# FNet/gMLP encoder layer on eight cores: earlier release of the first w_in cast and of group 1's x, row scales half a step back in the A loops, channel blocks moved on, one more merge add on VectorE

## The chip, the cores and the metric

One Trainium2 chip, 8 cores, each running the same program on its own sequences (cores 0 to 3: one prompt sequence of 2048 positions and one sample sequence of 4096; cores 4 to 7: three prompt sequences of 2048). No core talks to another. The metric is the device time in microseconds (us) of the slowest core; the outputs have to agree with the reference.

## What is computed

One layer of a trunk, cut to what matters here (per sequence of S positions, D = 1024):

```python
mod = silu(c) @ w_ada + b_ada                  # "adaLN": (B, 3D)
shift, scale, gate = split(mod, 3)
h = rmsnorm(x, norm_g) * (1 + scale) + shift
z = h @ w_in                                   # 4608 columns
a, ga, u, v, gb, ma, mb = split(z)             # 512 each, ma and mb 1024 each
y_a = fourier(a) * silu(ga)                    # real part of a 2-D DFT over (positions, 128 channels), 128x128 map per group
y_b = u * chunk_mix(layernorm(v)) * silu(gb)   # w_s over 128 positions
merged = sigmoid(ma) * (y_a @ w_pa) + sigmoid(mb) * (y_b @ w_pb)
y = rmsnorm(x + gate * (merged @ w_out), final_g)
```

## The kernel before

All five instruction streams are written out by hand in one program order: a small scheduler (`Sched`) appends each operation to its engine's stream and adds the semaphore waits that its reads and writes of 512-byte granules ask for. An engine runs its own stream strictly in that order, so where an operation stands in the program decides what it can hold up. The DMA queues are the streams of SyncE (x, tables, Gd, outputs), ScalarE (w_ada, at the start) and GpSimd (every weight that is cast from float32 to bfloat16 on its way: w_in by sections `w_sec`, w_pa, w_pb, w_out).

Each core has 48 blocks of 128 rows for the Fourier branch ("A") and 12 tiles T = 0 to 11 of 512 rows for the rest.

**Start.** ScalarE issues w_ada as eight 1 MB blocks (kc 0 to 7, `wada_off`). SyncE loads the first four x blocks, then waits for a block of w_ada before it loads four more (L876). GpSimd waits for a block of w_ada before it casts section 0 of w_in (L376). TensorE multiplies the eight w_ada blocks in order (L885), transposes group 0 of x (`fe_t`, L447), and the modulation tables come out (L896, L899); `fe_e` (L460 on VectorE, L465 on ScalarE) writes hT of group 0.

**A loops.** `ABlock.body` runs over groups q of four row blocks j. For each: `a_proj` (eight matmuls L490, VectorE copies the result, L313), then the first DFT stage of the block before it (`pend`: one matmul L500, copy alternately on ScalarE and VectorE, L313 or L311, write to Gd by SyncE, L503). At j = 2 comes `fe(q+1)`: 32 transposes that read all four scaled rows of the next group, then `fe_e`. At j = 0 and j = 2 stand one `sc(n)` and one `sq(n)`. n counts half groups (two row blocks): `sq(n)` squares two rows on ScalarE (L421) and takes the reciprocal root on GpSimd (L408, L410); `sc(n)` scales the two rows on VectorE (L427) and then has SyncE load the next rows into the ring slots that it has read. Object A has 4 groups in its loop (and two more groups, 4 and 5, that feed tiles 0 and 1; `A.fe(5)` stands behind the loop), a ring of 8; A2 has 8 groups (and one more), a ring of 6, and runs after tile 3.

**Channel blocks.** The second DFT stage reads Gd back (`g2_load`, L523) and has 4 blocks for the first sequence (`s3s`, `s3_single`, L560, L568) and 8 for the others (`s3j`, `s3_joint`, L535, L545). They are placed between the products of `silu_section` of the tiles (L680, Silu on ScalarE, L708) by its argument `between`. After tile 0's GA section `channel_tables` (L381 to L395) reads tables that `late_tabs` loads on SyncE's queue behind the reads of Gd; the casts of w_in sections 6, 7, 8, w_pa, w_pb and w_out follow on GpSimd's queue.

**Merge.** For each of eight blocks dmc `merge` makes two products (L772, L778), two multiplies on VectorE (L775, L781) and an add (L783): on GpSimd for dmc 0 to 6, on VectorE for dmc 7. In tile 1 and in tiles 4 and 8, GpSimd also multiplies the rows of w_out by the gate (`gate_mul`, L675) during the merge. `out_chunk` (L607) needs all eight merged blocks and all of w_out.

Of the kernel before, what the change touches and what calls it, by code (L numbers as in the profile page):

```python
# [210 lines left out]
def build_nc():  # L211
# [163 lines left out]

    w_sec(0, after=gk(wada_off[6], 512))  # L376

# [389 lines left out]

    def merge(tb, dmc):
        sl = tb.sigs.pop(dmc)
        mk = gk(tb.m + 1024 * dmc, 1024)  # L770
        b = newbank()
        S.pe([lambda e, k=k: e.matmul(ps[b][:], lhsT=w_pa_sb[:, k, dmc * 128:(dmc + 1) * 128], rhs=tb.sga[:, k, :],  # L772
                                      start=(k == 0), stop=(k == 3)) for k in range(4)],
             reads=gk(tb.a, 4096) + wpak, writes=[("ps", b)])
        S.op("dve", lambda e: e.tensor_tensor(out=tb.mg[:, dmc, :], in0=ps[b][:], in1=bv(sl[0], 512), op=ALU.mult),  # L775
             reads=[("ps", b)] + gk(sl[0], 1024), writes=mk)
        b2 = newbank()
        S.pe([lambda e, k=k: e.matmul(ps[b2][:], lhsT=w_pb_sb[:, k, dmc * 128:(dmc + 1) * 128], rhs=tb.sgb[:, k, :],  # L778
                                      start=(k == 0), stop=(k == 3)) for k in range(4)],
             reads=gk(tb.b, 4096) + wpbk, writes=[("ps", b2)])  # L780
        S.op("dve", lambda e: e.tensor_tensor(out=bv(sl[1], 512), in0=ps[b2][:], in1=bv(sl[1], 512), op=ALU.mult),  # L781
             reads=[("ps", b2)] + gk(sl[1], 1024), writes=gk(sl[1], 1024))
        S.op("pool" if dmc < 7 else "dve", lambda e: e.tensor_tensor(out=tb.mg[:, dmc, :], in0=tb.mg[:, dmc, :], in1=bv(sl[1], 512), op=ALU.add),  # L783
             reads=mk + gk(sl[1], 1024), writes=mk)


    class ABlock:
# [46 lines left out]
        def body(self, hooks):  # L834

            for q in range(self.nq):
                for j in range(4):
                    if j == 2:
                        self.fe(q + 1)
                    st1 = a_proj(self.dst[q][0], j, self.f, 4 * q + j, self.N1)  # L840
                    if self.pend:
                        self.pend.pop(0)()
                    self.pend.append(st1)
                    if j % 2 == 0:
                        self.sc(2 * q + j // 2 + 4)
                        self.sq(2 * q + j // 2 + 5)
                if q in hooks:
# [28 lines left out]
    tabs = []  # L876
    A.load_to(8, after=gk(wada_off[7], 512))
    for n in range(2):
# [27 lines left out]
    A.sc(2)  # L906
    A.sq(4)
    A.sc(3)
    A.body(hooks1)

    def s3_begin(f):
# [25 lines left out]
    silu_section(T0, SEC["GB"], T0.sgb, T0.b)  # L937
    silu_section(TB1, SEC["GB"], TB1.sgb, TB1.b, lambda fc: s3s(fc // 2) if fc % 2 == 0 else None)
    silu_section(T0, SEC["GA"], T0.sga, T0.a, lambda fc: s3s(2 + fc // 2) if fc % 2 == 0 else None)
    channel_tables()  # L940
# [3 lines left out]
    w_sec(8)  # L944
    silu_section(TB1, SEC["GA"], TB1.sga, TB1.a)
    w_out_load()
# [25 lines left out]
    for dmc in range(8):  # L972
        if dmc + 1 < 8:
            merge_gates(TB1, dmc + 1)
        merge(TB1, dmc)
        if dmc < 7:
# [27 lines left out]
    for T in range(2, NT):  # L1004
# [32 lines left out]
        after(0)  # L1037
        silu_section(tb, SEC["GB"], tb.sgb, tb.b, s3j if T == 4 else None)
        after(1)
        silu_section(tb, SEC["GA"], tb.sga, tb.a, (lambda fc: s3j(4 + fc)) if T == 4 else None)  # L1040
        after(2)
# [15 lines left out]
        for dmc in range(8):  # L1057
            if dmc + 1 < 8:
                merge_gates(tb, dmc + 1)
            if t == 0 and dmc < 7:  # L1060
                for k in ((0, 1) if dmc == 0 else (dmc + 1,)):
                    gate_mul(O_WIN, k)
            merge(tb, dmc)
            if T == 2 and dmc < 5:
# [40 lines left out]
        elif isA:  # L1105
            A2.fe(0)
            A2.sq(3)
            out_chunk(tb, T, 0, OS[0])
            A2.sc(3)
            A2.sq(4)  # L1110
            out_chunk(tb, T, 1, OS[1])
# [140 lines left out]
```

How the kernel before makes its waits and increments, by code:

```python
        def run(stream, e):  # L1130
            for it in stream:
                if it[0] == "wait":
                    e.wait_ge(sems[it[1]], it[2])
                elif it[0] == "raw":
                    it[1](e)
                else:
                    ins = it[1](e)
                    ins.then_inc(sems[it[2]], it[3])
```

## Time and profile before

| what | value |
|---|---|
| timed runs of the kernel | 1278.76, 1279.31, 1287.62 us, median 1279.31 |
| profiled execution | 1272.01 us, its span 1270.5 us (core 7, the slowest; the others 1264.0 to 1269.6) |
| busy, core 7 | PE 1222.7 us (96%), DVE 627.7 (49%), ACT 483.2 (38%), POOL 349.5 (28%) |
| mean granted TensorE clock | 0.992 to 0.995 of full on all cores |
| HBM | 143 MB read, 31 MB written, 138 GB/s over the span |

PE is TensorE's matmuls, PEld its weight loads, DVE VectorE, ACT ScalarE, POOL GpSimd, SP SyncE; a name with q (SPq) is the engine's queue, where DMAs are issued. The span runs from the first to the last instruction; the time of an execution is a little longer. A matmul's duration in the rows holds some 0.17 us of pipeline behind its last column, so the next one starts before it ends. L680 is line 680 of the kernel.

### The profile page before, as it was taken

Reading aid. Unit: us, or ns where it says so; the run is one execution under the profiler, and the core shown is the slowest. Engines: PE = TensorE matmul, PEld = TensorE weight load, DVE = VectorE, ACT = ScalarE, POOL = GpSimd, SP = SyncE. Lnnn points to the kernel's source line nnn. Section 1 sums busy time; section 2 is a strip of 40 time slices with the busy share of each in tenths; the row PEclk is TensorE's granted clock in tenths of the full one; section 3 lists DMA queues with packets and bytes.
Section 4 is the critical chain, followed back from the end, with each engine's and each line's share of the span. In section 5 each row is a group of like instructions: output and inputs, shape, how many; then the busy total and the mean of one; then the engine's idle time right before and its main releaser. Section 6 shows DMA issues by size and latency. Waiting matters only on the chain.

```text
span 1270.5 us, 19981 instructions; the slowest of 8 cores (1264.0 to 1270.5 us)
## 1 busy us (share of the span) xinstructions
PE 1222.7 (96%) x6504; PEld 587.9 (46%) x6504; DVE 627.7 (49%) x945; ACT 483.2 (38%) x818; POOL 349.5 (28%) x430
## 2 busy tenths in 40 slices
PE   6798999999999999989999999999999999999997
PEld 1354454444444455545444444444444444444443
DVE  0383265364756578844435434443446444344434
ACT  1483312323423368743332333243323423333322
POOL 0221132730522332203713213213128122132121
PEclk9899999999999999999999999999999999999999
DMA  8999895234426297656312212121262112121111
GB/s 273 265 254 186 167 170 164 67 116 147 156 80 208 77 302 266 194 164 137 100 50 67 84 50 84 67 90 60 84 136 86 72 62 95 50 84 67 64 70 67
DMA packets 57331, 158.21 MB, mean 125 GB/s; under 512 B 6026, under 2 KB 18698, under 8 KB 56078
## 3 DMA queue, kind: packets, MB, share of 16 engines
q1 hardware_dynamic: 46814, 130.58, 31.2%
q0 software_dynamic: 9120, 17.96, 9.2%
q10 hardware_dynamic: 1296, 8.40, 1.9%
q8 instruction: 54, 0.88, 0.3%
q14 instruction: 47, 0.39, 0.1%
HBM read 143.41 MB, written 31.47 MB: 138 GB/s over the span
## 4 chain that ended last, share of the span: by engine, by line
PE 84%; DMA 8%; DVE 2%; POOL 2%; issue 2%; ACT 1%; ACTq 0%; SPq 0%; DVEq 0%; POOLq 0%
PE ps L680 42%; PE ps L607 13%; PE ps L490 6%; PE ps L778 6%; PE ps L772 6%; PE ps L690 5%; PE ps L447 3%; DMA arena<-w_ada 2%; DMA arena<-Gd 2%; DMA arena<-w_out 2%; DMA arena<-xA 1%; POOL arena L783 1%; POOL arena L675 1%; DMA Gd<-arena 1%; PE ps L500 1%
## 5 line engine op out<-in xcount | busy, mean ns | idle before, releaser
L680 PE MATMUL ps<-arena 128*128 128x512 bf16 x2688 | 602.6, 380 | 2.4 <-DVE arena L729 1.7
L680 PEld LDWEIGHTS ps<-arena 128*128 128x128 bf16 x2688 | 262.1, 98 | 318.3 <-issue 8.0
L764 ACT ACTIVATE arena<-ps 128x512 bf16<-128x512 f32 x192 | 113.2, 596 | 282.8 <-PE ps L680 257.6
L783 POOL TENSOR_TENSOR arena<-arena 128x512 bf16<-128x512 bf16 x84 | 116.3, 1384 | 248.5 <-DVE arena L781 248.5
L775 DVE TENSOR_TENSOR arena<-ps,arena 128x512 bf16<-128x512 f32 x96 | 66.3, 691 | 223.1 <-PE ps L772 223.1
L607 PE MATMUL ps<-arena 128*128 128x512 bf16 x768 | 171.3, 379 | 4.0 <-DVE arena L783 1.5
L408 POOL TENSOR_TENSOR stat<-stat,eps_sb 128x1 f32<-128x1 f32 (+1 forms) x114 | 29.2, 256 | 380.9 <-ACT arena L615 298.6
L612 DVE TENSOR_TENSOR arena<-ps,arena 128x512 f32<-128x512 f32 x96 | 66.0, 691 | 126.8 <-PE ps L607 126.8
L607 PEld LDWEIGHTS ps<-arena 128*128 128x128 bf16 x768 | 74.6, 98 | 93.2 <-issue 5.5
L427 DVE TENSOR_SCALAR arena<-arena,stat 128x1024 bf16<-128x1024 f32 x96 | 81.6, 876 | 60.1 <-POOL stat L410 59.8
L421 ACT ACTIVATE arena<-arena 128x1024 bf16<-128x1024 f32 x96 | 101.2, 1054 | 22.9 <-DMA arena<-xA 16.9
L615 ACT ACTIVATE arena<-arena 128x1024 bf16<-128x1024 f32 x48 | 50.7, 1057 | 136.4 <-DVE arena L612 136.3
L772 PE MATMUL ps<-arena 128*128 128x512 bf16 x384 | 98.5, 379 | 0.0
L778 PE MATMUL ps<-arena 128*128 128x512 bf16 x384 | 98.5, 379 | 0.0
L490 PE MATMUL ps<-arena 128*128 128x512 bf16 x384 | 92.1, 384 | 4.4 <-DMA arena<-w_in 4.3
L313 DVE CAST arena<-ps 128x512 bf16<-128x512 f32 (+1 forms) x114 | 65.0, 606 | 52.1 <-PE ps L560 20.1
L690 PE MATMUL ps<-arena 128*128 128x512 bf16 x384 | 84.7, 379 | 0.0
L465 ACT ACTIVATE arena<-ps,modT,Gtab 128x512 bf16<-128x512 bf16 x96 | 66.8, 776 | 39.0 <-PE ps L447 35.1
L410 POOL TENSOR_TENSOR stat<-stat,mh_sb 128x1 f32<-128x1 f32 (+1 forms) x114 | 72.2, 633 | 16.7 <-POOL stat L408 0.7
L734 POOL TENSOR_TENSOR arena<-arena 128x512 bf16<-128x512 bf16 x48 | 53.8, 1151 | 73.2 <-DVE arena L729 73.2
L781 DVE TENSOR_TENSOR arena<-ps,arena 128x512 bf16<-128x512 f32 x96 | 66.3, 691 | 15.0 <-PE ps L778 9.8
L621 DVE SCALAR_TENSOR_TENSOR arena<-arena,stat 128x1024 f32<-128x1024 f32 x48 | 60.7, 1280 | 23.2 <-POOL stat L410 23.2
(80 smaller groups left out, 936.9 us busy)
## 6 DMA issues: line engine op xcount, KB each, us to landing
arena<-xB SPq DMA_DIRECT2D x96, 512.0 KB, 4.4
arena<-xA SPq DMA_DIRECT2D x48, 512.0 KB, 6.3
yu<-arena SPq DMA_DIRECT2D x48, 512.0 KB, 2.8
arena<-w_ada SPq DMA_DIRECT2D x24, 512.0 KB, 5.6
arena<-w_in POOLq DMA_DIRECT2D x9, 1024.0 KB, 17.9
arena<-w_ada ACTq DMA_DIRECT2D x8, 1024.0 KB, 23.7
Gd<-arena SPq DMA_DIRECT2D x48, 128.0 KB, 5.0
arena<-Gd SPq DMA_DIRECT2D x12, 512.0 KB, 8.1
```

Of the source, the lines that this page charges most:

```text
L410: S.op("pool", lambda e: e.tensor_tensor(out=dst, in0=dst, in1=mh_sb[:, 0:n], op=ALU.pow), reads=wk + ["mh"], writes=wk)
L421: S.op("act", lambda e: e.activation(out=junk, in_=fv(XS[k], 1024), func=AF.Square, scale=0.03125, accum_out=stat[:, 0, si:si + 1]), reads ...
L427: S.op("dve", lambda e: e.tensor_scalar(out=xr, in0=fv(XS[k], 1024), scalar1=stat[:, 1, si:si + 1], scalar2=None, op0=ALU.mult), reads=gk( ...
L465: S.op("act", lambda e, b=b, kk=kk, kc=kc: e.activation(out=hT[:, kc, :], in_=psb(b)[:, kk * 512:(kk + 1) * 512], func=AF.Identity, scale= ...
L490: S.pe([lambda e, kc=kc: e.matmul(ps[b][:], lhsT=hT[:, kc, j * 128:(j + 1) * 128], rhs=w_in_sb[:, 0, kc, :], start=(kc == 0), stop=(kc == ...
L607: S.pe([lambda e, b=b, dmc=dmc, half=half: e.matmul(ps[b][:], lhsT=tb.mg[:, dmc, j * 128:(j + 1) * 128], rhs=w_out_sb[:, dmc, half * 512:( ...
L680: S.pe([lambda e, kc=kc: e.matmul(ps[b][:], lhsT=w_in_sb[:, sec, kc, col:col + 128], rhs=tb.hT[:, kc, :], start=(kc == 0), stop=(kc == 7)) ...
L690: S.pe([lambda e, kc=kc, b=b, j=j: e.matmul(ps[b][:], lhsT=tb.hT[:, kc, j * 128:(j + 1) * 128], rhs=w_in_sb[:, SEC["V"], kc, :], start=(kc ...
L764: S.op("act", lambda e, b=b, so=so: e.activation(out=bv(so, 512), in_=ps[b][:], func=AF.Sigmoid), reads=[("ps", b)], writes=gk(so, 1024))
L772: S.pe([lambda e, k=k: e.matmul(ps[b][:], lhsT=w_pa_sb[:, k, dmc * 128:(dmc + 1) * 128], rhs=tb.sga[:, k, :], start=(k == 0), stop=(k == 3 ...
L778: S.pe([lambda e, k=k: e.matmul(ps[b2][:], lhsT=w_pb_sb[:, k, dmc * 128:(dmc + 1) * 128], rhs=tb.sgb[:, k, :], start=(k == 0), stop=(k == ...
L783: S.op("pool" if dmc < 7 else "dve", lambda e: e.tensor_tensor(out=tb.mg[:, dmc, :], in0=tb.mg[:, dmc, :], in1=bv(sl[1], 512), op=ALU.add) ...
```

## The change

Five edits.

1. w_in section 0's cast waits for w_ada block 5 instead of 6, the loads of group 1's x wait for block 6 instead of 7.
2. In `ABlock.body`, `sc` and `sq` take one half group less (n + 3 and n + 4 instead of n + 4 and n + 5); the `sc(3)` and `sq(4)` that stood before each loop are dropped, and `A.sc(11)` is put behind A's loop.
3. `s3s` blocks 0 to 3: from fc 0, 2 of tile 1's GB and fc 0, 2 of tile 0's GA to fc 3 of tile 1's GB, fc 1 and 3 of tile 0's GA and fc 1 of tile 1's GA (behind `channel_tables`).
4. `s3j` blocks 0 to 7 in tile 4: one product later each, and blocks 6 and 7 together behind the last product of GA.
5. `merge` has an argument: in tile 1 and in tiles 4 and 8 the add of dmc 6 too is on VectorE.

```diff
-    w_sec(0, after=gk(wada_off[6], 512))
+    w_sec(0, after=gk(wada_off[5], 512))
...
-    def merge(tb, dmc):
+    def merge(tb, dmc, nadd=7):
...
-        S.op("pool" if dmc < 7 else "dve", lambda e: e.tensor_tensor(out=tb.mg[:, dmc, :], in0=tb.mg[:, dmc, :], in1=bv(sl[1], 512), op=ALU.add),
+        S.op("pool" if dmc < nadd else "dve", lambda e: e.tensor_tensor(out=tb.mg[:, dmc, :], in0=tb.mg[:, dmc, :], in1=bv(sl[1], 512), op=ALU.add),
...
                     if j % 2 == 0:
-                        self.sc(2 * q + j // 2 + 4)
-                        self.sq(2 * q + j // 2 + 5)
+                        self.sc(2 * q + j // 2 + 3)
+                        self.sq(2 * q + j // 2 + 4)
...
-    A.load_to(8, after=gk(wada_off[7], 512))
+    A.load_to(8, after=gk(wada_off[6], 512))
...
     A.sc(2)
-    A.sq(4)
-    A.sc(3)
     A.body(hooks1)
+    A.sc(11)
...
-    silu_section(TB1, SEC["GB"], TB1.sgb, TB1.b, lambda fc: s3s(fc // 2) if fc % 2 == 0 else None)
-    silu_section(T0, SEC["GA"], T0.sga, T0.a, lambda fc: s3s(2 + fc // 2) if fc % 2 == 0 else None)
+    silu_section(TB1, SEC["GB"], TB1.sgb, TB1.b, lambda fc: s3s(0) if fc == 3 else None)
+    silu_section(T0, SEC["GA"], T0.sga, T0.a, lambda fc: s3s(1 + fc // 2) if fc % 2 else None)
...
-    silu_section(TB1, SEC["GA"], TB1.sga, TB1.a)
+    silu_section(TB1, SEC["GA"], TB1.sga, TB1.a, lambda fc: s3s(3) if fc == 1 else None)
...
-        merge(TB1, dmc)
+        merge(TB1, dmc, 6)
...
-        silu_section(tb, SEC["GB"], tb.sgb, tb.b, s3j if T == 4 else None)
+        silu_section(tb, SEC["GB"], tb.sgb, tb.b, (lambda fc: s3j(fc - 1) if fc else None) if T == 4 else None)
         after(1)
-        silu_section(tb, SEC["GA"], tb.sga, tb.a, (lambda fc: s3j(4 + fc)) if T == 4 else None)
+        silu_section(tb, SEC["GA"], tb.sga, tb.a, (lambda fc: (s3j(3 + fc), s3j(7) if fc == 3 else None)) if T == 4 else None)
...
-            merge(tb, dmc)
+            merge(tb, dmc, 6 if t == 0 else 7)
...
             out_chunk(tb, T, 0, OS[0])
-            A2.sc(3)
-            A2.sq(4)
             out_chunk(tb, T, 1, OS[1])
```

## Rows read from the trace of the kernel before

**Rows 1.** The waits, TensorE, whole span: us in total, times, longest.
```profile
PE ps L500 <- DVE arena L313: 5.3, 3, 3.2
PE ps L560 <- DMA arena<-Gd: 5.3, 2, 2.7
PE ps L490 <- DMA arena<-w_in: 4.3, 1, 4.3
PE ps L535 <- DMA arena<-Gd: 2.5, 1, 2.5
```

**Rows 2.** Busy time by stretch: engines, then PEclk, DMA share, GB/s.
```profile
34.00:41.00 7.00, 7.00 (x18) 1.37 (x16) 1.58 (x3) 0.00 (x0) 3.29 (x5) 1.00 0.52 179
...
170.00:172.00 2.00, 1.55 (x10) 1.08 (x11) 2.00 (x5) 0.00 (x0) 1.39 (x2) 0.70 1.04 169
...
564.00:566.00 2.00, 2.00 (x6) 0.69 (x5) 2.00 (x7) 1.27 (x4) 0.00 (x0) 0.50 0.82 257
...
984.00:987.00 3.00, 1.63 (x14) 0.86 (x12) 2.35 (x5) 2.42 (x4) 1.54 (x2) 1.00 0.90 366
```

**Rows 3.** The timeline, start: start us, duration us, engine, line, operation, idle before.
```profile
33.46 10.46 PE L885 MATMUL ps<-arena,cs_sb 128*3 128x512 f32 x24 [0.32 <-DMA arena<-w_ada]
...
38.80 20.75 SPq L403 DMA_DIRECT2D arena<-xA  x12
...
47.66 2.78 ACT L465 ACTIVATE arena<-ps,modT,Gtab 128x512 bf16<-128x512 bf16 x4 [3.92 <-DVE Gtab L899]
...
51.23 5.32 PE L490 MATMUL ps<-arena 128*128 128x512 bf16 x16 [4.35 <-DMA arena<-w_in]
...
55.15 1.06 ACT L421 ACTIVATE arena<-arena 128x1024 bf16<-128x1024 f32 x1 [0.83 <-DMA arena<-xA]
...
57.58 1.42 DVE L427 TENSOR_SCALAR arena<-arena,stat 128x1024 bf16<-128x1024 f32 x2 [1.86 <-POOL stat L410]
...
59.95 1.95 PE L447 MATMUL ps<-arena 128*128 128x128 bf16 x32
```

**Rows 4.** The timeline, one group of the A2 loop.
```profile
517.99 1.29 DVE L313 CAST arena<-ps 128x512 bf16<-128x512 f32 x2 [0.67 <-PE ps L490]
...
519.19 1.41 DVE L427 TENSOR_SCALAR arena<-arena,stat 128x1024 bf16<-128x1024 f32 x2
...
519.80 1.95 PE L447 MATMUL ps<-arena 128*128 128x128 bf16 x32
```

**Rows 5.** The timeline, end of the first A loop.
```profile
96.61 1.95 PE L447 MATMUL ps<-arena 128*128 128x128 bf16 x32
96.95 0.69 DVE L313 CAST arena<-ps 128x512 bf16<-128x512 f32 x1 [0.70 <-PE ps L500]
```

**Rows 6.** The timeline around the channel tables.
```profile
139.73 1.06 PE L560 MATMUL ps<-arena 128*128 128x128 bf16 x16
...
141.88 0.43 DVE L390 CAST arena<-arena 128x512 bf16<-128x512 f32 x1 [0.30 <-DMA arena<-final_g]
142.35 0.38 PE L381 MATMUL ps<-arena 128*128 128x128 f32 x2
```

**Rows 7.** The timeline, end of tile 1's merge.
```profile
259.94 1.84 DVE L783 TENSOR_TENSOR arena<-arena 128x512 bf16<-128x512 bf16 x1
...
261.75 13.97 PE L607 MATMUL ps<-arena 128*128 128x512 bf16 x64 [1.00 <-POOL arena L675]
```

**Rows 8.** The timeline, tile 4, GB section.
```profile
563.39 3.52 PE L680 MATMUL ps<-arena 128*128 128x512 bf16 x8 [0.57 <-ACT arena L311]
```

**Rows 9.** The chain that ended last: start us, us, what.
```profile
132.09 3.45 PE ps L680 x16
```

**Rows 10.** The timeline, end of tile 8's merge.
```profile
983.74 0.79 DVE L783 TENSOR_TENSOR arena<-arena 128x512 bf16<-128x512 bf16 x1
984.21 1.33 POOL L783 TENSOR_TENSOR arena<-arena 128x512 bf16<-128x512 bf16 x1
985.80 4.48 PE L607 MATMUL ps<-arena 128*128 128x512 bf16 x20 [1.37 <-POOL arena L783]
```

## The prediction

> **What bounds the kernel now.** I read the page's busy table first: TensorE is busy for 1222.7 of 1270.5 us, so in nearly the whole span only its own work counts, and an edit can win no more than the 48 us in which it is idle. So I went to TensorE's waits [rows 1]. Behind the w_ada products there are few: 5.3 us on VectorE's copies in three places (3.2 in one, at 59.7), 5.3 us on reads of Gd for the channel blocks of the first sequence, 4.3 us on w_in at 51.2, 2.5 us on Gd in tile 4. In the A loops from group 2 on there is nothing: there TensorE sets the pace, and whatever delays it is paid in full. Then the stretches by DMA share: between 34 and 41 us the DMA engines are busy only 0.52 of the time [rows 2], while from 41 to about 141 us they are full. Then the timeline of each place that the edits touch.
>
> **Edit 1, the start.** Now w_ada block 7 lands at 38.8, when SyncE issues x of group 1, and nothing new flows before [rows 3]. The hole in the DMA is 0.48 x 7 = 3.4 us. After the change the cast starts when block 5 lands (33.5) and x at some 37: the hole is filled. What TensorE gets from it is less. The w_ada products end at 43.9 (33.46 + 10.46) and hT of group 0 is ready at 50.44 (47.66 + 2.78), so the first `a_proj` moves from 51.23 to 50.5 at best. The transposes of group 1 (59.95) hang on the squares of its four rows. The last one ends now at 56.2; ScalarE can't begin them before hT is written, and four of about 1.25 us with their accumulator reads give 55.4, so 0.8 to 0.9 us. Edit 2 adds here that the copy of `a_proj(0)` no longer stands behind `sc(3)` on VectorE: now scale (ends 59.00), copy, L500, transposes at 59.95; afterwards the transposes follow the scale directly, 0.1 us behind it, 0.8 us more. Both ends: 1.7 us won, or nothing, if w_ada block 7 comes late (rival 2). I take 1.2. On the queues: GpSimd's first reciprocal roots stand behind the cast's issue and come 3.6 us earlier, which no one waits for; SyncE's later loads only start earlier.
>
> **Edit 2, the scales.** Each `sc` now stands where the previous one stood, so `fe(q+1)` at j = 2 needs the `sc` issued at j = 0 of the same step. On VectorE this one comes behind two copies: 517.99 + 1.29, then the scale from 519.19 to 520.60 [rows 4]. TensorE reaches the transposes at 519.80. In the changed kernel that same VectorE slot holds the scale that they read, so they start at 520.60 + 0.14 = 520.74: a pause of 0.94 us in every group. VectorE can't do it sooner, since it is in order and the copy before it waits for the `a_proj` that ends at 517.8. Nothing hides it; TensorE's next work all stands behind the transposes. The pause doesn't grow: VectorE and ScalarE have idle time in each step and shift along with TensorE.
> A2: 8 groups, 8 x 0.94 = +7.5 us. A: groups 1 to 3, 3 x 0.94 = +2.8 us. The bounds of one pause are 0.4 and 1.4 (the scale's place in the queue moves by one copy at most). `A.sc(11)` behind A's loop: `fe(5)` starts now at 96.61; the scale will come behind the last copy on VectorE (96.95 + 0.69 = 97.64 [rows 5]), takes 1.41, and the transposes start at 99.15: +2.5 us. The loads which each `sc` and each `sq` issue or use keep their distance (three half steps with the ring of 8, two with the ring of 6), so I cost them at nothing. The dropped `sc(3)` and `sq(4)` ahead of A2 stood beside w_out products: nothing.
> Behind `fe(5)` TensorE is then -1.2 + 2.8 + 2.5 = +4.1 us late.
>
> **Edit 3, first channel blocks.** One product group is 8 matmuls, 3.45 / 2 = 1.73 us [rows 9]. Block 0 moves behind three more of them (5.2 us), block 1 behind as many, so both waits for Gd go, 5.3 us [rows 1]. What is late next is `channel_tables`. Its tables land just in time now: VectorE still waits for the last of them at 141.88, and TensorE starts at 142.35 [rows 6]. TensorE would arrive at 142.35 + 4.1 - 5.3 - 1.1 (block 3, 1.06 us, is now behind it) = 140.05. The tables are the end of a DMA backlog that begins at 41 us; with the hole of 3.4 us filled they land between 138.5 (all of it kept) and 142.0 (nothing). I take 140.3, so the tables start at 140.4, 1.95 us earlier, and with block 3's 1.06 us done later the stage ends 0.9 us earlier than before, all of edits 1 to 3 in A together (between -1.2 and +0.9). Block 3 delays the w_out casts on GpSimd's queue by a few us; their readers come 70 us later.
>
> **Edit 4, tile 4.** The wait for Gd is 2.46 us [rows 1]; one product (1.73) now stands ahead of it, 0.7 is left: -1.7. The pauses in this place also bring the clock down: at 564 to 566 us it is 0.50 (1.2 GHz) [rows 2], and a group of 8 takes 3.52 instead of 1.73 us [rows 8]. If the clock stays up that is another 1.8, and ScalarE's copies, spread better, may give 1 more. Between -1.7 and -4.5, I take -3.0. Blocks 6 and 7 next to each other need 1.06 us each of TensorE as before, and the U products behind them cover their copies.
>
> **Edit 5, the adds.** Tile 1: `out_chunk` waits 1.00 us for GpSimd's last gate multiply [rows 7], which stood behind the add of dmc 6: -1.0. Tile 8: it waits 1.37 us for that add itself [rows 10], but here the last multiply stands ahead of the merge and runs when VectorE gets to the add. A VectorE add beside such a multiply isn't short: 1.84 us [rows 7] and 0.79 us [rows 10], each ending about when GpSimd is done (984.2 in tile 8). So the add of dmc 6 ends at about 984.5, and two multiplies of 0.69, their hand-over and the last add (0.42) stand behind it: 986.4, against 985.5 for GpSimd's add now, and with the pipeline of the last waits I take +0.7 us (if the add took its bare 0.42 us: -1.4). Tile 4 has no such wait: 0.
> The Trainium skill ("SBUF — State Buffer", section "SBUF: two separate sides") says why it should be so: VectorE and GpSimd share one port pair under an exclusive lock for the whole instruction, and whoever comes second blocks. Rows 7 and 10 agree. By that rule the sum is as here; with a free add it would be 2.1 us lower.
>
> **The sum.** -0.9 (to the tables) - 1.0 + 7.5 - 3.0 + 0.7 = +3.3 us. Against the profiled execution: 1272.0 + 3.3 = 1275.3. The timed runs lie higher, with a median of 1279.3; the same difference on it gives 1282.6.
>
> **Rivals.**
> 1. The transposes don't wait, because VectorE gets to the scale earlier than I read. For it: VectorE is idle for 0.67 us in front of the copies. Against: that idle time is a wait for TensorE, and the order is fixed. Then A2 costs nothing, the tables still hold TensorE at 140.4, and the sum is 3.3 - 7.5 = -4.2: 1275.
> 2. The early cast takes DMA time from w_ada blocks 6 and 7. TensorE needs block 7 at 40.4 (the last third of the 10.46 us), it lands by 38.8. From 34 to 41 us the DMA does 0.52 x 7 = 3.6 us of full work [rows 2]; of w_ada some 2.4 us of that (my estimate) is left at 34.4, when the cast has been issued. With half of the engines it lands at 39.9, in time; with a third, beside the cast and x, at 42.3, 1.9 us late. Then TensorE reaches the tables at 141.95, after they land, and the sum rises by 1.6 to +4.9: 1284. The Trainium skill ("DMA: Bandwidth & Descriptors", section "Queues, rings and completion order") has each DMA engine go round between the queues that have work; that is the third. The hole at 34 to 41 can't show it.
> 3. The add on VectorE is free beside GpSimd: 1.2 instead of 3.3, 1280.5. Against: rows 7 and 10.
> 4. Slower: the clock. If each pause in front of the transposes brings TensorE down to 1.2 GHz, the 16 matmuls behind it take 5.32 us, as at 51.23 [rows 3], instead of 3.45 [rows 9] and 0.17 of pipeline: 1.7 us for each of 11 pauses, 18.7 us on top of the 3.3: 1301. It decides from six falls in A2 (10.2 + 3.3 us, over 1%). For it: between 170 and 172 us, with TensorE busy for 1.55 of 2 us, the clock is 0.70. Against: with the pause of 1.37 us at 984 to 987 it stayed at 1.00 [rows 2], and full product groups stand around the pauses here.
> 5. The hole in the DMA isn't filled, because x comes no earlier: tables at 142.0, sum +5.1: 1284.
>
> **Chances.** Forecast 0.60, rival 1 0.12, rival 2 0.10, rival 3 0.08, rival 4 0.04, rival 5 0.06. About 1% (12.8 us) is what a measurement of this kernel can tell from no change; only rival 4 goes past it, and a chance of 0.02 is left for what I don't see on the other side. So faster 0.02, same 0.94, slower 0.04. The forecast's terms alone (A2 6 to 8.5, tables -1.2 to +0.9, tile 4 -4.5 to -1.7, adds -2.4 to 0) span -2 to +7; rival 1 is taken in at the low end, and two us for the scatter of runs at the high end: 1275 to 1289.
>
> **What would show it.** TensorE's waits should have a new row, L447 <- VectorE L427, 12 to 13 times, some 0.9 us each and 2.5 in one place; the rows L560 <- Gd gone and a wait of TensorE or VectorE for the tables at 140; A2's loop 7.5 us longer from its first `a_proj` to the V products of tile 4; L535 <- Gd at 0.7 us; L607 <- POOL L675 gone and L607 in tile 8 waiting for VectorE's add. DMA share near 1 between 34 and 41. I am wrong if that L447 row is missing, or if the clock column shows falls between 465 and 545 us.

## The result, and the profile after

The changed kernel takes 1288.35 us (median of 8 runs), the kernel before beside it on the same chip 1281.9 us (median of 6). In some executions of any kernel one die runs at a lower clock and takes several per cent longer; medians and ratios here and below are of the other executions. The ratio is 1.0049, with a 95% interval of 1.0027 to 1.0071: some 6.3 us slower, where the forecast had +3.3 us. The interval is far narrower than the 1% I had taken for what a measurement can tell, so a change of 0.5% shows.

The cores, before and then after: span and mean granted clock.

```profile
die 0 (median of its cores): 1267.8 us, clock 0.992
die 1 (median of its cores): 1266.8 us, clock 0.993
```

```profile
core 0: 1287.7 us, clock 0.981
...
core 7: 1277.1 us, clock 0.992
die 0 (median of its cores): 1283.0 us, clock 0.985
die 1 (median of its cores): 1275.6 us, clock 0.992
```

The profiled execution took 1289.27 us. Cores 0 to 3 have stretches at a granted clock of 0.81 that no core of the kernel before has, nor cores 4 to 7 here. So I compare core 7 with core 7, which the forecast was read from: 1270.5 before, 1277.1 after, +6.6 us. Core 7 was the longest before and has the smallest difference of all eight: the other cores of its die are 7.5 to 10.1 us longer, cores 0 to 3 9.2 to 18.3 us. That +6.6 is so close to the +6.3 of the timed runs is therefore chance. Those go by the slowest core, which is one of cores 0 to 3 in all eight runs of the changed kernel; the cores of the timed runs before are not on record, and these runs (1278.8 to 1287.6 us) lie above the profiled 1272.0 for a reason that isn't known.

TensorE's waits on core 7 after the change, whole span (total us, times, longest), to set beside [rows 1]:

```profile
PE ps L447 <- DVE arena L427: 12.9, 13, 2.6
...
PE ps L490 <- ACT arena L465: 3.8, 1, 3.8
PE ps L607 <- DVE arena L783: 3.5, 2, 2.0
...
PE ps L535 <- DVE arena L313: 0.7, 1, 0.7
```

The new row is there, 13 times. L560 <- Gd and L535 <- Gd are gone; in tile 4 the channel blocks wait 0.7 us for VectorE's copies instead of 2.5 for Gd. L607 <- L783 is VectorE's adds ahead of the output products: 1.99 us of it are new, in tile 8; the other 1.54, in tile 11, stood there before too. The timeline of one A2 group after, against [rows 4]:

```profile
519.72 1.29 DVE L313 CAST arena<-ps 128x512 bf16<-128x512 f32 x2 [0.67 <-PE ps L490]
...
520.93 1.41 DVE L427 TENSOR_SCALAR arena<-arena,stat 128x1024 bf16<-128x1024 f32 x2
...
522.48 1.95 PE L447 MATMUL ps<-arena 128*128 128x128 bf16 x32 [0.78 <-DVE arena L427]
```

The same VectorE slots stand as far apart as before (1.21 us from copies to scale); only now TensorE waits for the scale: its transposes start 1.55 us behind it, where before they ran beside it.

The start and the end of the first A loop on core 7, against [rows 3] and [rows 5]:

```profile
49.28 5.30 PE L490 MATMUL ps<-arena 128*128 128x512 bf16 x16 [3.81 <-ACT arena L465]
...
56.94 1.95 PE L447 MATMUL ps<-arena 128*128 128x128 bf16 x32 [1.81 <-DVE arena L427]
...
95.61 0.38 PE L500 MATMUL ps<-arena 128*128 128x512 bf16 x1 [1.37 <-DVE arena L313]
...
96.77 1.54 DVE L427 TENSOR_SCALAR arena<-arena,stat 128x1024 bf16<-128x1024 f32 x2
...
98.56 3.57 PE L447 MATMUL ps<-arena 128*128 128x128 bf16 x32 [2.57 <-DVE arena L427]
```

The last line is what I had not priced: the 32 transposes of `fe(5)` take 3.57 us instead of 1.95. The stretches on core 7 (busy time of TensorE, its weight load, VectorE, ScalarE, GpSimd; then granted clock, DMA share, GB/s):

```profile
34.00:41.00 7.00, 6.99 (x17) 1.32 (x16) 2.94 (x5) 0.59 (x1) 1.85 (x3) 1.00 1.02 249
...
94.00:96.00 2.00, 0.62 (x3) 0.10 (x1) 1.47 (x3) 1.11 (x3) 1.03 (x3) 1.00 0.85 118
96.00:98.00 2.00, 0.00 (x0) 0.00 (x0) 1.83 (x3) 0.00 (x0) 2.00 (x3) 0.81 1.05 150
98.00:100.00 2.00, 1.44 (x14) 1.47 (x15) 0.56 (x2) 0.00 (x0) 1.17 (x2) 0.50 1.10 240
100.00:102.00 2.00, 2.00 (x22) 2.00 (x20) 1.29 (x4) 1.42 (x2) 0.00 (x0) 0.50 1.12 229
```

Two waits in a row (1.37 and 2.57 us) leave TensorE idle for most of 94 to 98 us, and the clock goes to 0.50, the lower level of 1.2 GHz. All eight cores show this, between 97 and 107 us; before, none does between 66 and 124 us. The 1.37 us wait alone does not bring it: it stood ahead of `fe(5)` before too (1.38 at 96.4 us), and the clock stayed at 1.00. The first line is edit 1: the DMA share of 34 to 41 us went from 0.52 to 1.02.

Where the time went on core 7, by the starts of the stages in the timelines:

| stretch of core 7 | forecast | measured |
|---|---|---|
| to tile 0's first output product (261.75, now 258.81) | -1.9 | -2.9 |
| A2, to its last transposes (77.48 long, now 84.96) | +7.5 | +7.5 |
| tile 4, first V product to tile 5's (94.66, now 93.40) | -3.0 | -1.3 |
| tile 8, to tile 9's first V product (89.4, now 92.8) | +0.7 | +3.4 |
| all else | 0 | 0 |
| sum | +3.3 | +6.7 |

### The profile page after: what moved, and what is told of

Same layout as the page of the kernel before. It is cut to its first block, busy times and chain, and to the rows that moved or that the text cites. A ratio compares the mean times of both kernels' runs of the same rounds, so it can differ in the third digit from the quotient of the medians.

```text
span 1287.7 us, 19865 instructions; the slowest of 8 cores (1272.4 to 1287.7 us)
## 1 busy us (share of the span) xinstructions
PE 1228.8 (95%) x6389; PEld 592.8 (46%) x6504; DVE 633.1 (49%) x948; ACT 483.4 (38%) x818; POOL 345.6 (27%) x427
## 4 chain that ended last, share of the span: by engine, by line
PE 89%; DVE 4%; issue 2%; DMA 2%; ACT 1%; ACTq 0%; POOL 0%; DVEq 0%; POOLq 0%
PE ps L680 45%; PE ps L607 13%; PE ps L778 7%; PE ps L772 7%; PE ps L690 6%; PE ps L490 4%; PE ps L447 4%; DMA arena<-w_ada 2%; DVE arena L427 1%; DVE arena L313 1%; PE ps L885 1%; DVE arena L621 1%; DVE arena L729 1%; PE ps L723 1%; PE ps L535 0%
## 5 line engine op out<-in xcount | busy, mean ns | idle before, releaser
L783 POOL TENSOR_TENSOR arena<-arena 128x512 bf16<-128x512 bf16 x81 | 112.9, 1394 | 247.7 <-DVE arena L781 247.7
L607 PE MATMUL ps<-arena 128*128 128x512 bf16 x735 | 167.9, 379 | 5.7 <-DVE arena L783 4.1
L607 PEld LDWEIGHTS ps<-arena 128*128 128x128 bf16 x768 | 74.6, 98 | 92.9 <-issue 5.9
L734 POOL TENSOR_TENSOR arena<-arena 128x512 bf16<-128x512 bf16 x48 | 53.8, 1150 | 74.8 <-DVE arena L729 74.6
```

Of the source, the lines that this page charges most:

```text
L607: S.pe([lambda e, b=b, dmc=dmc, half=half: e.matmul(ps[b][:], lhsT=tb.mg[:, dmc, j * 128:(j + 1) * 128], rhs=w_out_sb[:, dmc, half * 512:( ...
L783: S.op("pool" if dmc < nadd else "dve", lambda e: e.tensor_tensor(out=tb.mg[:, dmc, :], in0=tb.mg[:, dmc, :], in1=bv(sl[1], 512), op=ALU.add),
```

## Experiments

Each batch had its own runs of the kernel before, with medians of 1273.1 (e1 to e4), 1275.4 (e5 to e8) and 1274.9 us (e9 to e12). Timed runs go by the slowest of eight cores; to find the place of a gain I also read the same marks in every core's timeline. The table has the median over the eight cores of each stage's length, in us. "tile 4" is here from the first channel-block product in it to tile 5's first V product, "tables" the first product of `channel_tables`.

```
kernel            ratio    to 1st  to     A     fe(5)  V to    A2    tile  tile 8
                           a_proj  fe(1)  loop  to V   tables        4     (all cores)
before                     50.3    8.8    37.0  1.8    42.3    77.5  84.3  88.4 (87.6-90.2)
after             1.0049   50.4    7.7    41.9  3.4    38.9    85.3  83.1  89.6 (88.7-92.8)
e1_scales_back    0.9994   50.2    8.5    36.9  1.8    41.6    77.5  81.4  89.8 (87.6-92.3)
e2_scales_only    1.0068   50.7    8.2    42.3  3.4    39.3    85.0  82.7  89.2
e3_scale_first    1.0025   50.1    8.5    39.8  3.3    38.9    80.4  81.8  88.3
e4_t8_add_pool    1.0051   50.1    7.7    41.6  3.2    39.8    84.9  82.4  88.2
e5_tabs_first     1.0010   50.8    8.5    36.1  1.8    51.3    77.5  79.0  89.9
e6_wout_halves    0.9958   52.0    8.0    36.1  1.8    42.6    77.5  80.9  87.6 (all)
e7_sc11_ahead     1.0085   51.1    7.2    40.8  3.0    42.0    85.0  82.2  90.5
e8_start_only     0.9988   50.7    8.5    36.1  1.8    44.8    77.5  83.9  90.1
e9_halves_t4      0.9950   50.8    8.1    36.1  1.8    43.0    77.5  79.2  87.6
e10_no_start      -        51.1    8.9    37.1  1.8    41.8    77.5  78.8  87.6
e11_final_g_later 0.9933   50.9    8.3    36.1  1.8    41.1    77.5  78.5  87.6
e12_halves_only   0.9984   51.0    8.6    37.7  1.8    44.2    77.5  84.3  87.6 (all)
```

Each row is one profiled execution. Up to the tables the columns scatter: the kernel before and e12 have the same program up to the w_out cast behind the tables, and still their tables stand at 140.2 and 144.6 us on the median core. A difference of a few us up to there decides nothing by itself. A2 is the same to 0.1 us on the median core of every kernel with the scales in their old places.

The theory was that edit 2, with its one late scale per group, is the loss, and that the rest of the change is worth a little; the rivals were that it is the clock or the tile 8 add.

**e1_scales_back**: the changed kernel with edit 2 undone.

```
-                        self.sc(2 * q + j // 2 + 3)
-                        self.sq(2 * q + j // 2 + 4)
+                        self.sc(2 * q + j // 2 + 4)
+                        self.sq(2 * q + j // 2 + 5)
...
+    A.sq(4)
+    A.sc(3)
     A.body(hooks1)
-    A.sc(11)
...
+            A2.sc(3)
+            A2.sq(4)
```

> The changed kernel with edit 2 alone undone (scales and squares where they were). Theory: the scales are what the change loses by. Then TensorE's row L447 <- DVE L427 is gone, the A2 loop is 7.5 us shorter than in the changed kernel, fe(5) starts 1.4 us or less behind the last product and the clock doesn't fall there; all in all 10 to 14 us less than the changed kernel, 3 to 7 us less than the kernel before. Rival: the loss sits in tile 8 and in the pair of first tiles; then at most 4 us less than the changed kernel, and still slower than before.

Measured: 0.9994 (0.9984 to 1.0004). A2 and the A loop are back at 77.5 and 36.9 us and the fall behind `fe(5)` is gone, but the other four edits together win nothing that shows, where 3 to 7 us were expected. One reason is what takes the place of the Gd wait. Core 4's waits between 98 and 145 us, first of the kernel before, then of e1:

```profile
PE ps L560 <- DMA arena<-Gd: 2.2, 1, 2.2
```

```profile
PE ps L381 <- DMA arena<-final_g: 5.3, 1, 5.3
```

TensorE waits at the tables instead, 1.8 to 5.4 us on all eight cores, and behind that wait the granted clock falls to 0.50 on five of them (0, 2, 4, 5 and 6, between 138 and 146 us), which it does on no core before. Another is tile 8, 1.4 us longer on the median core, which takes back half of what tile 4 wins (2.9 us). The Gd wait itself was 5.3 us on core 7, but 4.0, 2.7, 2.2 and 2.0 on cores 5, 2, 4 and 0: the forecast had read one core.

**e2_scales_only**: the kernel before with edit 2 alone (the diff of e1 the other way round).

> The kernel before with edit 2 alone. Theory: 12 to 13 waits L447 <- DVE L427 of 0.8 us each and one of 2.5; A2 +7.5 us, behind fe(5) +5 us and up to 3.4 us more where the clock falls; of this first part a few us are taken back at the reads of Gd, so +10 to +14 us over the kernel before. Rival (the pauses are worth little because something else sets the end): under +4 us.

Measured: 1.0068 (1.0047 to 1.0089). A2 +7.5, A loop +5.3, `fe(5)` to the first V product +1.6, and -3.0 up to the tables, which wait less the later TensorE comes. By the ratio it is 8.7 us, at least as much as the whole change loses, and e1 without it loses nothing: e1 and e2 together settle that edit 2 is the whole loss.

**e3_scale_first**: after, with each `sc` ahead of the half step's `a_proj`.

```
                     if j % 2 == 0:
+                        self.sc(2 * q + j // 2 + 3)
+                    st1 = a_proj(...)
...
-                        self.sc(2 * q + j // 2 + 3)
```

> The changed kernel with each scale of the A loops put ahead of the a_proj beside it instead of behind it: the same scale in the same half step, but on VectorE ahead of the two copies. Theory (the place behind the two copies makes the pause): no wait L447 <- DVE L427 in the A2 loop, each group back to 9.56 us, some 10 us less than the changed kernel; the one wait of 2.5 us at fe(5) stays, because that scale stands behind the loop. Rival (the half step itself is too little time for square, root and scale): the wait stays at 0.5 to 1 us per group, now because the scale waits for GpSimd's root.

Measured: 1.0025 (1.0016 to 1.0034). The pause is not gone but smaller: A2 is 80.4 us, (80.4 - 77.5) / 8 = 0.36 us for each group instead of 0.94. A group of core 7:

```profile
528.80 0.69 DVE L313 CAST arena<-ps 128x512 bf16<-128x512 f32 x1 [0.63 <-PE ps L490]
...
530.56 1.42 DVE L427 TENSOR_SCALAR arena<-arena,stat 128x1024 bf16<-128x1024 f32 x2 [1.08 <-POOL stat L410]
531.90 1.88 DVE L313 CAST arena<-ps 128x512 bf16<-128x512 f32 x3
...
532.72 0.38 PE L500 MATMUL ps<-arena 128*128 128x512 bf16 x1 [0.22 <-DVE arena L313]
```

The scale, issued earlier, now waits 1.08 us for GpSimd's reciprocal root, and the copies behind it are late in their turn. So the half step that edit 2 took away cannot be made up by the order on VectorE alone: the statistics are only just ready.

**e4_t8_add_pool**: after, with tile 8's add of dmc 6 on GpSimd again.

```
-            merge(tb, dmc, 6 if t == 0 else 7)
+            merge(tb, dmc, 6 if T == 4 else 7)
```

> The changed kernel, with the add of dmc 6 in tile 8 alone back on GpSimd. Theory (VectorE's add blocks beside GpSimd's gate multiply): the wait in front of tile 8's w_out products falls from 2.0 to 1.4 us, the VectorE add of 2.08 us is gone, and the clock fall behind it too, 1.7 us more: 2.3 us less in tile 8. Rival (the late landing of w_out sets tile 8's end in either case): tile 8 within 0.5 us of the changed kernel's.

Measured: 1.0051 (1.0036 to 1.0066), beside 1.0049 for after in another batch: the add is a small term. On cores where the cast lands late, tile 8's first output product stands 30.8 us behind its first gate multiply with the VectorE add (e1 core 1: 52.1 and 82.92; after core 5: 53.0 and 83.79, us into the tile) and 30.2 with GpSimd's (before core 7: 52.3 and 82.50; e4 core 1: 52.2 and 82.44): +0.6 us. From there to tile 9's first V product the clock decides: where it falls behind the adds, the way from the first gate multiply to that product is 39.4 us instead of 37.7. That happens on two cores of after, two of e1 and three of e5, all with the VectorE add, and on none of before, e2, e4 and e8, which have GpSimd's. But other cores of e1, e3 and e7 have the same wait of 2.0 us for the VectorE add and no fall. On the median core tile 8 is 1.4 us shorter than in after (88.2 for 89.6), where 2.3 were expected.

**e5_tabs_first**: e1 with `late_tabs()` ahead of `s3_begin(1)`, and in tile 4 the copies of the first channel blocks all on VectorE.

```
     pair = (T0, TB1)
+    late_tabs()
     s3_begin(1)
...
-    late_tabs()
...
-            eng = ("act", "dve")[g % 2]
+            eng = "dve" if blk < 2 else ("act", "dve")[g % 2]
```

> e1 (the change without edit 2) with two parts more: the tables of late_tabs are loaded ahead of the reads of Gd instead of behind them, and the copies of s3j blocks 0 and 1 in tile 4 are all on VectorE. Theory for the first (in e1 the 3.9 to 5.4 us that TensorE waits for the tables at L381 are the old waits for Gd, moved): that wait is gone on every core, channel_tables starts 3 to 5 us earlier than in e1 and at most 1 us of waits for Gd comes back. Rival (the DMA backlog as a whole sets it): the wait moves to L560 <- Gd at the same size. For the second (behind the wait for Gd, ScalarE's chain of V copies, table load, Silu and copies is what holds tile 4): the stage from the first s3j to tile 5's V products shrinks from 81.4 by 1.5 to 3 us, and the clock doesn't fall there. Together 4 to 7 us under the kernel before.

Measured: 1.001 (0.9999 to 1.0021). Core 0's waits between 90 and 150 us:

```profile
PE ps L560 <- DMA arena<-Gd: 13.0, 1, 13.0
```

With the tables ahead of Gd in the queue it is Gd that comes late, and the stage grows from 41.6 to 51.3 us: the order only moves the wait, as the rival said, and makes it longer. The 4 to 7 us that were expected did not come. Tile 4, on the other hand, is 2.4 us shorter than in e1.

**e6_wout_halves**: e1, with the w_out cast's two halves on two semaphores, and tile 8's add on GpSimd.

```
-        S.dma("pool", [lambda e, k=k: e.dma_start(...) for k in range(2)], "s_wout", writes=woutk)
+        for k in range(2):
+            S.dma("pool", [lambda e, k=k: e.dma_start(...)],
+                  ("s_wout", "s_wout2")[k], writes=gk(O_WOUT + 8192 * k, 8192))
```

> e1 with the cast of w_out on one semaphore for each half instead of one for both, and tile 8's add of dmc 6 back on GpSimd. Theory (the late landing of w_out's second half lets GpSimd's gate multiplies in tile 8 start 48 to 54 us into the tile, and the end of the tile follows that time): they start 6 to 9 us earlier, TensorE doesn't wait at tile 8's w_out products on any core, and tile 8 is 87.6 us on all cores instead of 87.6 to 92.8. Rival (GpSimd's and VectorE's chain in the merge is too slow in itself): the wait stays at about 1 us.

Measured: 0.9958 (0.9943 to 0.9974). Tile 8 on core 7, the kernel before and then e6:

```profile
934.16 1.59 POOL L670 DMA_DIRECT2D arena<-w_out  x2
...
955.59 4.23 POOL L675 TENSOR_TENSOR arena<-arena 128x1024 bf16<-128x1024 bf16 x2 [10.31 <-DMA arena<-w_out]
```

```profile
932.95 1.58 POOL L671 DMA_DIRECT2D arena<-w_out  x2
...
944.91 4.23 POOL L676 TENSOR_TENSOR arena<-arena 128x1024 bf16<-128x1024 bf16 x2 [0.84 <-DMA arena<-w_out]
```

The gate multiplies of the first half no longer wait for the second half's landing: 10.31 us of GpSimd's idle time become 0.84. On single cores before, the first multiply stood 48.4 to 53.1 us into the tile, here 41.9 to 43.9, and tile 8 takes 87.6 us on all eight. In the other kernels its length is set by when w_out lands, and varies by core.

**e7_sc11_ahead**: after, with the last scale issued at j = 3 of the last group instead of behind the loop.

```
+                    if q == self.nq - 1 and j == 3:
+                        self.sc(2 * q + 5)
...
-    A.sc(11)
```

> The changed kernel with sc(11) one place ahead: behind the copy of a_proj(3,3), ahead of the last first-stage block, instead of behind the loop. Theory (the idle time of nearly 4 us around fe(5) brings the clock down): the wait at fe(5) falls from 2.6 to about 1 us, the clock stays at 1.00 between 95 and 105 us, and from fe(5) to the first V product it takes 1.8 us again instead of 3.4; 3 us less than the changed kernel up to there, part of it given back at the tables. Rival (the pauses at the transposes of every group are what brings the clock down): the clock falls as before.

Measured: 1.0085 (1.0057 to 1.0113), from three runs. The wait on core 7 shrinks from 2.57 to 1.79 us:

```profile
97.16 0.38 PE L500 MATMUL ps<-arena 128*128 128x512 bf16 x1 [1.37 <-DVE arena L313]
...
97.53 1.55 DVE L427 TENSOR_SCALAR arena<-arena,stat 128x1024 bf16<-128x1024 f32 x2 [0.51 <-POOL stat L410]
...
99.33 1.95 PE L447 MATMUL ps<-arena 128*128 128x128 bf16 x32 [1.79 <-DVE arena L427]
```

The clock from 98 to 104 us stays at 1.00 on cores 4, 6 and 7, where the stage behind `fe(5)` takes 1.8 to 2.0 us; it is 0.50 to 0.72 on the five others, and the median stage is 3.0 instead of 3.4 us. So the fall belongs to the idle time around `fe(5)` and can be lost by some 0.8 us of it, but not reliably. The ratio is no better than after's, and the stages say where the gain goes: TensorE now waits 2.4 to 6.3 us for `final_g` at the tables on seven cores, the clock falls to 0.50 there on the same seven, and the median stage up to the tables is 42.0 us instead of 38.9.

**e8_start_only**: the kernel before with edit 1 alone.

> The kernel before with edit 1 alone. Theory: the DMA share between 34 and 41 us goes from 0.52 to 1, the transposes of group 1 start some 1 us earlier (0.8 of the 1.7 needs edit 2's order), and the reads of Gd and the tables land up to 3 us earlier, so channel_tables starts 1 to 3 us earlier than before. Rival (early cast robs w_ada blocks 6 and 7): first a_proj later by up to 2 us, channel_tables no earlier.

Measured: 0.9988 (0.9977 to 0.9999). The tables start at 142.3 us on the median core, before at 140.2, so not the 1 to 3 us earlier that were expected: what is early at the first V product is waited for again (V to tables 44.8 us for 42.3). The hole in the DMA is filled here too, with w_ada unhurt (core 0):

```profile
34.00:41.00 7.00, 7.00 (x18) 1.37 (x16) 2.83 (x4) 0.00 (x0) 3.02 (x5) 1.00 1.03 257
```

**e9_halves_t4**: e6 with tile 4's copies of e5, and **e10_no_start**: the same without edit 1.

> e6 (the change without edit 2, w_out's cast in two halves, tile 8's add on GpSimd) with the copies of s3j blocks 0 and 1 in tile 4 on VectorE. Theory (stages add up): tile 4's stage falls from 80.9 to 79 us as in e5, the rest is e6; 2 us under e6, ratio to the kernel before 0.994 to 0.996. Rival: within 0.5 us of e6, because what tile 4 gains is lost at the next wait.

> e9 without edit 1. Theory (filling the DMA's hole brings the tables earlier): channel_tables starts 1 to 3 us later than in e9. Rival (as e8 hints, where filling it did nothing for the reads of Gd): no later than in e9, within 1 us.

Measured: e9 0.995 (0.9932 to 0.9968). For e10 there is no ratio, so only its stages count: the transposes of group 1 start 1.4 us later than in e9 (60.3 against 58.9), and the tables at 141.1 against 140.8. The 1.4 us are no longer there at the tables, as the rival said; a difference of 0.3 us is far inside the scatter of this column. Core 4 of e9 in tile 4:

```profile
555.95 10.23 DVE L313 CAST arena<-ps 128x256 bf16<-128x256 f32 x26 [2.40 <-PE ps L535]
```

```profile
562.00:564.00 2.00, 2.00 (x17) 1.06 (x15) 2.00 (x8) 1.38 (x5) 0.00 (x0) 1.00 0.63 197
```

VectorE now has the channel blocks' copies while ScalarE loads its table and does the Silu, and the clock stays at 1.00, as on seven of the eight cores.

**e11_final_g_later**: e9 with the load of `final_g` taken out of `late_tabs()` and put behind the gate loads.

```
-        tab(fg_bc, dram_ap(final_g, 0, [[0, 128], [1, D]]))
...
     gate_load(1, 1)
+    S.dma("sp", [lambda e: e.dma_start(out=fg_bc, ...)], "s_fg", writes=["fg"])
```

> e9 with the load of final_g (512 KB, the last and largest of the tables, not used before the first outputs) on a semaphore of its own behind the first gate loads, so that channel_tables doesn't wait for it. Theory (in e1, e6 and e9 the tables' landing holds TensorE at L381, the last bytes being final_g's): the wait at L381 falls from about 4 to 2 us and the stage up to tile 0's outputs is 2 us shorter. Rival (GpSimd's casts behind channel_tables are what is late next): the wait falls, but the stage isn't shorter.

Measured: 0.9933 (0.9914 to 0.9952), 1265.6 us (three runs): faster than both kernels, by some 8.5 us against the one before. The wait at the tables is not gone (core 4, 98 to 146 us):

```profile
PE ps L380 <- DMA arena<-b_s: 5.7, 1, 5.7
```

It has another last load, but the stage is 1.9 us shorter than in e9. That less of the backlog stands ahead of the tables would explain it, but this is argued: the same program differs by as much from run to run (42.3 in the kernel before, 44.2 in e12), and the intervals of e9 and e11 overlap.

**e12_halves_only**: the kernel before with the w_out halves of e6 alone.

> The kernel before with w_out's cast in two halves, nothing of the change. Theory (tile 8's length in the kernel before, 87.6 to 90.2 us by core, is the landing of w_out): 87.6 us on all cores, 1 to 3 us less on the slowest core; ratio 0.998 to 0.999. Rival: as the kernel before.

Measured: 0.9984 (0.9974 to 0.9994). Tile 8 is 87.6 us on all cores, 0.8 us less than the median before and 2.6 less than the longest. So of e11's gain the halves are about a quarter; tile 4 is 5.8 us of the median core's stages (84.3 to 78.5).

## Why the prediction was right or wrong

The time of 1288.35 us lies inside the stated 1275 to 1289, but by luck: the forecast was 1282.6, the kernel before alone ran 2.6 us above the 1279.3 that it was added to, and the change was twice the forecast. Beside the +7.5 of A2 the sum had -4.2 us for everything else; it was -0.9 on core 7 (6.6 - 7.5) and -1.2 by the timed runs (6.3 - 7.5). The steps that failed are the two terms of tile 4 (-3.0, measured -1.3) and tile 8 (+0.7, measured +3.4), the clock behind `fe(5)`, which was priced at nothing (+1.6), one core's wait for Gd taken for all of them, and the bound of 1% for what a comparison can tell, which turned a forecast loss into "no change".

**Right: edit 2 in A2.** Forecast 8 x 0.94 = +7.5 us; +7.5 on core 7, +7.5 alone in e2, gone in e1. Of the 12.9 us on the new row, 1.81 are at the start and 2.57 at `fe(5)`; the other 11 are (12.9 - 1.81 - 2.57) / 11 = 0.77 us each, and the rest of the 0.94 is the pipeline's. Rival 1, that the transposes don't wait, falls with the row. Rival 4, the clock, falls for A2: from 462 to 550 us cores 4 to 7 have a granted clock of 1.00 throughout, and so have all eight cores of e2.

**Right in size, but the clock priced at nothing: the A loop.** "TensorE is then ... +4.1 us late" behind `fe(5)`. The loop is +4.9 (after) or +5.3 (e2) long for a forecast of 2.8 + 2.5 = 5.3. But the step took only the delay of `fe(5)` and not what two waits in a row do to the clock: from `fe(5)` to the first V product it is 3.4 us instead of 1.8, +1.6. I had looked for the clock only as a rival in all 11 pauses or none, and 2.5 us of wait with 1.37 ahead of it is another case than 0.94. My reading that from group 2 on nothing waits in the A loops overlooks the 1.38 us at 96.4, which is the first of these two waits. On core 7 the +1.6 is hidden in the sum, because the start was 1.8 us better than forecast.

**Right number for core 7 by luck, wrong for the chip: edit 3.** Forecast 140.4 us for the tables' start; 140.33. But the forecast had the tables land last, at 140.3. They landed at 138.9 on core 7 (issued at 129.20, 9.7 us to landing), and neither TensorE nor VectorE waits for them:

```profile
129.20 0.45 SPq L338 DMA_DIRECT2D arena<-final_g  x1
...
140.33 0.44 PE L381 MATMUL ps<-arena 128*128 128x128 f32 x2
```

TensorE is busy without a gap from 101.93 to 140.33: it set the time itself. That this comes out at the forecast is the better start and the slower clock behind `fe(5)`, which about cancel. The predicted wait for the tables is missing on seven of the eight cores (core 3 has 1.6 us). The term also rests on the 5.3 us of [rows 1], which on other cores are 2.0 to 4.0. The median core has its tables 2.1 us later than before (142.3 against 140.2), not 2.0 earlier, though this column scatters by as much. e1 shows the cap that I had described: with TensorE early it waits for `final_g`. Rival 5, that the hole isn't filled, falls: the DMA share of 34 to 41 us is 1.02.

**Right: the start.** Forecast -1.2 us up to the transposes of group 1; median -1.2, core 7 -3.0, of which 1.4 is that its w_ada products ended earlier in this execution (42.43 for 43.85). Rival 2 falls: TensorE's first `a_proj` came earlier on core 7 (49.28 for 51.23) and waited for ScalarE's hT, not for w_ada. Its landings of 39.9 and 42.3 us don't follow from 2.4 us of work left at 34.4 (that gives 39.2 and 41.6), which changes nothing here. Edit 1 alone is worth 0.0012 of the time (0.0001 to 0.0023), and nothing that shows by the tables.

**Wrong: the term of tile 4, "I take -3.0".** Measured -1.3 on core 7, -1.2 on the median. The wait for Gd went, and 0.7 us is left in its place, as worked out, though for VectorE's copies. What did not come on core 7 is the clock's 1.8, because a chain on ScalarE is next. Core 7 after:

```profile
560.34 2.79 ACT L701 ACTIVATE arena<-ps,bnag 128x512 bf16<-128x512 f32 x4 [10.29 <-DVE bnag L697]
...
563.14 1.28 ACT L708 ACT_TABLE_LOAD   x1
...
566.43 0.38 PE L535 MATMUL ps<-arena 128*128 128x128 bf16 x4 [0.37 <-ACT arena L311]
...
568.44 3.48 PE L680 MATMUL ps<-arena 128*128 128x512 bf16 x8 [0.57 <-ACT arena L311]
```

The V copies (2.79 us), the table load and the Silu stand ahead of the channel blocks' copies on ScalarE, TensorE waits for these twice, and its 8 matmuls still take 3.48 us as in [rows 8]: the clock does not stay up, which was 1.8 of my 3.0. The same short waits stand on every core of after and of e1, and the clock falls behind them on some only. In e1, with edit 4 as it is here, it falls on two cores (93.5 us from tile 4's first V product to tile 5's); on the other six it stays up and the stretch takes 91.8 us, 2.9 less than core 7 before: there the term is right. In after only core 6 has the 91.8. So the -3.0 took for certain what happens on some cores. With the copies on VectorE (e5, e9) these waits are gone and the stage is 5 us shorter than before, beyond the end of my range (-4.5), for a reason that this change does not bring.

**Wrong: the term of tile 8, +0.7.** The add is right: +0.6 by e4 and e1, and it took VectorE 2.08 us beside the last gate multiply, which ended at 988.62 (986.49 + 2.13), 0.28 us before the add:

```profile
986.49 2.13 POOL L675 TENSOR_TENSOR arena<-arena 128x1024 bf16<-128x1024 bf16 x1
986.82 2.08 DVE L783 TENSOR_TENSOR arena<-arena 128x512 bf16<-128x512 bf16 x1
...
990.77 8.75 PE L607 MATMUL ps<-arena 128*128 128x512 bf16 x32 [1.99 <-DVE arena L783]
```

Rival 3 falls with this row: the same add takes 0.43 us where no multiply runs beside it. The Trainium skill ("SBUF — State Buffer", section "SBUF: two separate sides") says that of VectorE and GpSimd the one that comes second to their shared ports is blocked for the other's whole instruction. This row agrees, as rows 7 and 10 did: VectorE starts 0.33 us behind GpSimd and ends behind it. But the stage is +3.4 us on core 7. Of it 0.6 is the add, some 1.1 the w_out cast that landed later, and 1.7 the output products, part of which ran at the lower clock level:

```profile
992.00:994.00 2.00, 2.00 (x6) 0.73 (x5) 0.64 (x2) 0.00 (x0) 0.00 (x0) 0.50 0.13 53
```

My step costed the edit from when the merge ends and took the merge's own beginning as fixed. It isn't: it hangs on a cast whose landing varies by core (the first gate multiply stands 48.4 to 53.1 us into the tile before, 50.2 to 54.0 after). e6 shows it by removing the wait: 87.6 us on all cores. So core 7's +3.4 is not the price of the edit: the median core has +1.2, and in e1, with the same add, core 7 takes 87.6 us. The 1.7 us at the low clock stand on seven cores in all and only with the VectorE add (see e4), but the same wait of 2.0 us also stands without them; what decides it is open.

**Right: tile 1.** The wait of [rows 7] for GpSimd is gone, -1.0:

```profile
256.43 1.21 DVE L783 TENSOR_TENSOR arena<-arena 128x512 bf16<-128x512 bf16 x1
...
258.81 3.40 PE L607 MATMUL ps<-arena 128*128 128x512 bf16 x15
```

**The balance.** On core 7 the errors are -1.0 (first part), +1.7 (tile 4) and +2.7 (tile 8), +3.4 on +3.3. The direction of the sum held, its size was half. The clock alone makes 3.4 us of these errors (1.7 in tile 4, 1.7 in tile 8); the others cancel. The chance of 0.94 for no change rested on a bound of 1%; the comparison resolves 0.22%, so a sum of +3.3 us (0.26%) already called for a forecast of slower.

## What to carry to other kernels

A producer moved half a step later is free only if its consumer stood more than that behind it: set the two starts of one period beside each other in the timeline (519.19 and 519.80 here), and multiply the difference by the number of periods. Before you count a wait as won, read it on every core, and ask which load or engine is next; here, with the scales in their old places, the wait for Gd that went came back at the next table, and in tile 4 at ScalarE. Where two casts share a semaphore, the first half's readers wait for both: a semaphore for each was the cheapest gain found (0.16% alone). And before you forecast "no change", look at how far the comparison resolves, not at how far single runs scatter.

## What was new about the hardware

- TensorE's clock fell to 0.50 on all eight cores where 1.37 and 2.57 to 2.72 us of waiting stood almost together (94 to 98 us on core 7); with 1.37 and 1.77 to 1.79 (e7) on five of the eight; with 1.38 alone (before), and with a pause of 0.8 us in every group of A2 (cores 4 to 7), not at all. Where it falls behind the same short waits on some cores only, one fall costs 1.7 us (tile 4: 91.8 or 93.5; tile 8: 37.7 or 39.4).
- In the kernel after, and in hardly any other (e3 has one each on cores 2 and 3), cores 0 to 3 show stretches at a granted clock of 0.81 while TensorE has work, 8 to 14 a core, none on cores 4 to 7. Core 0:

```profile
100.00:110.00 10.00, 8.91 (x53) 5.80 (x55) 4.19 (x8) 2.89 (x4) 0.92 (x2) 0.68 1.05 182
...
118.00:120.00 2.00, 2.00 (x9) 0.85 (x8) 0.88 (x2) 0.12 (x1) 0.00 (x0) 0.81 1.08 199
```

  The first line is the fall at `fe(5)`, the second such a stretch with TensorE fully busy. The timed runs list the same die at 0.979 to 0.989 against 0.990 to 0.995. e2 and e4, with the same scales, ran on another occasion and don't show it, so what brings it stays open.
- The same cast lands at different times on the eight cores of one program: w_out's readers started 48.4 to 53.1 us into tile 8 before and 50.2 to 54.0 after, and tile 8 was 87.6 to 90.2 and 88.7 to 92.8 us long, mostly for that reason.
